# Up pairs of the last feed-forward block in seven block products

## What is computed

```python
def swiglu(h, w_gate, w_up, w_down):
    return (jax.nn.silu(h @ w_gate) * (h @ w_up)) @ w_down

h = modulate(rms_norm(x, norm_ffn2[i]), sh3, sc3)
x = x + 0.5 * gt3[:, None, :] * swiglu(h, ffn2_gate[i], ffn2_up[i], ffn2_down[i])
```

## Time and profile before

| | |
|---|---|
| median of 3 runs | 1440.79 us (1439.36 to 1442.40) |
| profiled execution, whole | 1442.35 us |
| its span | 1440.7 us |
| PE busy, 11790 matmuls | 1391.4 us, 97% |
| DVE busy | 976.9 us, 68% |
| ACT busy | 539.3 us, 37% |
| POOL busy | 77.4 us, 5% |

### The profile page before, as it was taken

The page is one execution under the profiler, slowest core; times in us unless marked ns, Lnnn a source line. Parts: engine busy times, 40 slices in busy tenths (PEclk is TensorE's granted clock), DMA queues, the critical chain, the costliest instruction groups (busy, mean ns, idle before and its releaser), DMA issues.

```text
span 1440.7 us, 28804 instructions
## 1 busy us (share of the span) xinstructions
PE 1391.4 (97%) x11790; PEld 1346.0 (93%) x11790; DVE 976.9 (68%) x1731; ACT 539.3 (37%) x797; POOL 77.4 (5%) x118
## 2 busy tenths in 40 slices
PE   6999999999999999999999998999999999999996
PEld 5899999999998999999899897999899999999996
DVE  5446775357546588998998997854554786456745
ACT  5323343224336222524233236422342344224433
POOL 6100000010001000000000000000000000000000
PEclk8999999999999999999999999999999999999998
DMA  9754646455364223213334443626312242223221
GB/s 323 229 180 146 210 150 205 146 166 146 97 206 143 87 88 93 89 60 103 128 123 147 147 156 126 212 89 199 110 41 91 74 134 89 96 81 117 90 87 60
DMA packets 132701, 189.49 MB, mean 132 GB/s; under 512 B 4621, under 2 KB 112545, under 8 KB 132386
## 3 DMA queue, kind: packets, MB, share of 16 engines
q1 hardware_dynamic: 111388, 112.54, 24.7%
q0 software_dynamic: 17136, 66.87, 13.8%
q10 hardware_dynamic: 4070, 8.57, 1.6%
HBM read 173.73 MB, written 15.18 MB: 131 GB/s over the span
## 4 chain that ended last, share of the span: by engine, by line
PE 82%; DVE 11%; ACT 3%; DMA 2%; issue 2%; POOL 0%; DVEq 0%; ACTq 0%; POOLq 0%
PE pu L642 47%; PE pu L817 13%; PE pu L806 11%; PE pu L658 3%; PE pg L679 2%; DVE w_lo L1667 2%; DMA work<-in_w_ada 1%; ACT w_hi L1214 1%; PE pg L1052 1%; DVE d L2087 1%; PE pg L715 1%; PE pg L1116 1%; DMA raw_a<-in_w_ada 1%; DVE w_lo L1956 1%; DVE work L2197 1%
## 5 line engine op out<-in xcount | busy, mean ns | idle before, releaser
L1667 DVE TENSOR_TENSOR w_lo<-raw,w_hi 128x1024 fp32r<-128x1024 f32 x152 | 186.1, 1225 | 259.2 <-ACT w_hi L1214 259.0
L1214 ACT CAST w_hi<-raw 128x1024 fp32r<-128x1024 f32 x152 | 158.8, 1046 | 402.0 <-PE pu L642 360.6
L642 PE MATMUL pu<-h_hi,w_hi 128*128 128x260 f32 x1408 | 288.5, 286 | 5.2 <-DVE w_lo L1667 3.6
L642 PE MATMUL pu<-h_hi,w_lo 128*128 128x260 f32 x1408 | 284.0, 283 | 0.0
L642 PE MATMUL pu<-h_lo,w_hi 128*128 128x260 f32 x1408 | 283.6, 283 | 0.0
L642 PEld LDWEIGHTS pu<-h_hi,w_hi 128*128 128x128 f32 x1408 | 217.5, 189 | 9.0 <-DVE w_lo L1667 5.3
L642 PEld LDWEIGHTS pu<-h_lo,w_hi 128*128 128x128 f32 x1408 | 217.4, 189 | 0.0
L642 PEld LDWEIGHTS pu<-h_hi,w_lo 128*128 128x128 f32 x1408 | 217.4, 189 | 0.0
L2087 DVE SCALAR_TENSOR_TENSOR d<-u,cw,d 128x512 f32<-128x512 f32 x240 | 163.1, 743 | 0.1
L642 PE MATMUL pu<-f_hi,w_hi 128*128 128x260 f32 x704 | 143.1, 284 | 0.9 <-DVE f_lo L2028 0.9
L642 PE MATMUL pu<-f_hi,w_lo 128*128 128x260 f32 x704 | 141.8, 283 | 0.0
(11 more groups left out here) (349 smaller groups left out, 2372.0 us busy)
## 6 DMA issues: line engine op xcount, KB each, us to landing
raw_a<-in_w_ada POOLq DMA_DIRECT2D x30, 1024.0 KB, 7.9
raw<-in_w_in SPq DMA_DIRECT2D x28, 1024.0 KB, 5.2
raw<-in_ffn_up SPq DMA_DIRECT2D x22, 1024.0 KB, 5.3
raw<-in_ffn_gate SPq DMA_DIRECT2D x21, 1024.0 KB, 5.3
raw<-in_ffn_down SPq DMA_DIRECT2D x16, 1024.0 KB, 5.1
gates_d<-sg ACTq DMA_DIRECT2D x24, 260.0 KB, 2.2
raw<-in_ffn_down SPq DMA_DIRECT2D x8, 768.0 KB, 4.4
work<-gates_d POOLq DMA_DIRECT2D x2, 2080.0 KB, 8.6
```

The source lines that it names most:

```text
L642: last = mm(pu[p][:, e, 0:HALF], w[p][:, k, :], m[:, k, e * HALF:(e + 1) * HALF], start=(k == 0 and j == 0), stop=(k == k_tiles - 1 and j ...
L1214: nc.scalar.copy(w_hi[p][:], raw[:, slot, :, p * P:(p + 1) * P]).then_inc(s_hi, 1)
L1667: V.tensor_tensor(w_lo[p][:], raw[:, slot, :, p * P:(p + 1) * P], w_hi[p][:].bitcast(F32), ALU.subtract).then_inc(s_lo, 1)
```

## The change

In groups 1 and 2 of the last feed-forward block (`which == 2`) the up pair too is made of seven block products. A turn is then 14 blocks (`2 * PAIR`), 168 matmuls: the gate pair in the four banks of `pu`, the up pair in the four of `pg`. The first feed-forward block keeps its turns of 11. With it:

- Weight sums of up pairs, and of the gate pairs of turns 2 to 4 of a group, are made by POOL; those of a group's first gate pair stay with DVE. The second half of `w_sums` holds the up pair's sums.
- The up pair's parts and result lie in `lb`. POOL multiplies `lb` by `sg` (Silu of gate) when both are whole, in the turn after; ACT's cast and DVE's `f_lo` follow in positions 0 to 2 of the next turn. For the last turn of a group they come behind all blocks, and the down unit starts with `GROUPS[g] - 2` tiles ready.
- DVE's first half-width sum of a turn waits for both POOL products of the turn before (`s_um`). Slab loads wait for POOL's sums as well.
- `unit_pair` gets `together`: that many k tiles run for both units, then the rest for unit 0, then the rest for unit 1 (6 for conv and yconv, 5 for the last feed-forward block, 8 as before for the first).
- In the last gate-up unit of group 0, in both feed-forward blocks, DVE multiplies gate and up before it splits the next weights.
- In yconv's loop `o_low` works on the tile of the same step and `o_gated` on the next one; one of each is moved in front of the loop.

The core of the diff:

```diff
+        def first_block(t):
+            return TURN * t if t < FFN2_TURN else TURN * FFN2_TURN + 2 * PAIR * (t - FFN2_TURN)
+
+        def pair_no(t, up=0):
+            return t if t < FFN2_TURN else FFN2_TURN + 2 * (t - FFN2_TURN) + up
+
+        def raw_quarter(t, up, m2, k2):
+
+            m2 = m2 if t < FFN2_TURN else 1 - m2
+            return raw[:, up, 4 * k2:4 * k2 + 4, m2 * P:(m2 + 1) * P]
+
+        def block_source(t, pos):
+
+            up, q = divmod(pos, PAIR) if t >= FFN2_TURN else (0, pos)
+            if q in SUM_OF:
+                return w_sums[:, 1 - up, SUM_OF[q]], s_wsum, 4 * pair_no(t, up) + SUM_OF[q] + 1
+            if t < FFN2_TURN:
+                return raw_block(pos), (s_graw if pos < U0A else s_uraw), 16 * (t + 1)
+            m2, k2 = {P1: (0, 0), P2: (0, 1), P4: (1, 1)}[q]
+            return raw_quarter(t, up, m2, k2), (s_uraw if up else s_graw), 16 * (t + 1)
+
+        def sum_of_weights(t, up, k):
+
+            a11, a12, a21, a22 = (raw_quarter(t, up, m2, k2) for m2 in range(2) for k2 in range(2))
+            w = w_sums[:, 1 - up]
+            return ((w[:, 0], a21, a22, ALU.add), (w[:, 1], w[:, 0], a11, ALU.subtract),
+                    (w[:, 2], a11, a21, ALU.subtract), (w[:, 3], a12, w[:, 1], ALU.subtract))[k]
@@ SP @@
                         sp.dma_start(raw[:, 0], cols(wg, r0 + 256 * it)).then_inc(s_graw, 16)
                         if it == 0:
                             sp.wait_ge(s_lo, n0)
+                        elif which == 1:
+                            sp.wait_ge(s_blo, TURN * t)
                         else:
-                            sp.wait_ge(s_blo, TURN * t)
+                            sp.wait_ge(s_blo, first_block(t - 1) + PAIR + P4 + 1)
+                            sp.wait_ge(s_wsum, 4 * pair_no(t - 1, 1) + 4)
                         sp.dma_start(raw[:, 1], cols(wu, r0 + 256 * it)).then_inc(s_uraw, 16)
-                    sp.wait_ge(s_blo, TURN * t + P4 + 1)
+                    sp.wait_ge(s_blo, first_block(t) + P4 + 1)
+                    if which == 2:
+                        sp.wait_ge(s_wsum, 4 * pair_no(t) + 4)
                     load(Lin(n0), 0, cols(wd, 0, r0=r0))
-                    sp.wait_ge(s_blo, TURN * (t + 1))
+                    if which == 1:
+                        sp.wait_ge(s_blo, TURN * (t + 1))
+                    else:
+                        sp.wait_ge(s_blo, first_block(t) + PAIR + P4 + 1)
+                        sp.wait_ge(s_wsum, 4 * pair_no(t, 1) + 4)
                     load(Lin(n0 + 2), 1, cols(wd, 256, r0=r0))
                     pair(Lin(n0 + 4), wd, 512, r0=r0)
@@ POOL @@
+            def add_weights(t, up):
+
+                for k in range(4):
+                    pool.wait_ge(s_wsum, 4 * pair_no(t, up) + k)
+                    if k == 0:
+                        pool.wait_ge(s_uraw if up else s_graw, 16 * (t + 1))
+                        if t > FFN2_TURN:
+                            pool.wait_ge(s_blo, first_block(t) if up else first_block(t - 1) + P3 + 1)
+                    out, a, b, op = sum_of_weights(t, up, k)
+                    nc.gpsimd.tensor_tensor(out, a, b, op).then_inc(s_wsum, 1)
+
+            def hidden(t, k):
+
+                pool.wait_ge(s_sg, 2 * t + k + 1)
+                pool.wait_ge((s_c2, s_c12)[k], pair_no(t, 1) + 1)
+                nc.gpsimd.tensor_tensor(lb[:, 1 - k, :], lb[:, 1 - k, :], sg[:, 1 - k, :], ALU.mult).then_inc(s_um, 1)
+
+            for g in (1, 2):
+                for it, t in turns(2, g):
+                    if it == 0:
+                        add_weights(t, 1)
+                    if it + 1 < TURNS:
+                        add_weights(t + 1, 0)
+                    hidden(t, 0)
+                    hidden(t, 1)
+                    if it + 1 < TURNS:
+                        add_weights(t + 1, 1)
+
 
@@ PE @@
+            def unit_pair(n, hi, lo, s, v, between=None, together=KT):
 
 
                 for p in range(2):
                     weights_and_psum(n + p, p)
-                for k in range(KT):
+                def rows(p, k):
+
+                    pe.wait_ge(s, v + k + 1)
+                    for j, (w, m) in enumerate(((w_hi, hi), (w_hi, lo), (w_lo, hi))):
+                        for e in range(2):
+                            last = mm(pu[p][:, e, 0:HALF], w[p][:, k, :], m[:, k, e * HALF:(e + 1) * HALF],
+                                      start=(k == 0 and j == 0), stop=(k == KT - 1 and j == 2))
+                    if k == KT - 1:
+                        last.then_inc(s_done, 1)
+
+                for k in range(together):
                     if between is not None:
                         between(k)
-                    pe.wait_ge(s, v + k + 1)
                     for p in range(2):
-                        for j, (w, m) in enumerate(((w_hi, hi), (w_hi, lo), (w_lo, hi))):
-                            for e in range(2):
-                                last = mm(pu[p][:, e, 0:HALF], w[p][:, k, :], m[:, k, e * HALF:(e + 1) * HALF],
-                                          start=(k == 0 and j == 0), stop=(k == KT - 1 and j == 2))
-                        if k == KT - 1:
-                            last.then_inc(s_done, 1)
+                        rows(p, k)
+                for p in range(2):
+                    for k in range(together, KT):
+                        rows(p, k)
 
+            def pairs_of_blocks(g):
+
+
+                for it, t in turns(2, g):
+                    for up in range(2):
+                        q, j = pair_no(t, up), first_block(t) + PAIR * up
+                        a0, a1, b0, b1 = (pg[:, b, 0:HALF] if up else pu[b // 2][:, b % 2, 0:HALF] for b in range(4))
+                        first, used = it == 0 and not up, it > 0 or (up and g == 2)
+                        if first:
+                            pe.wait_ge(s_evac[0], at[f"down2_{g}"] // 2)
+                        if used:
+                            pe.wait_ge(s_u3, q - 1)
+                            pe.wait_ge(s_c2, q - 1)
+                        product(j + P1, a0, h_block(h_hi, 0, 0), h_block(h_lo, 0, 0))
+                        product(j + P2, a1, h_block(h_hi, 1, 0), h_block(h_lo, 1, 0))
+                        if first:
+                            pe.wait_ge(s_evac[1], at[f"down2_{g}"] // 2)
+                            pe.wait_ge(s_tl, 8)
+                        if used:
+                            pe.wait_ge(s_v2, q - 1)
+                            pe.wait_ge(s_c12, q - 1)
+                        product(j + P6, b0, t_hi[:, 1], t_lo[:, 1])
+                        product(j + P5, b1, t_hi[:, 0], t_lo[:, 0])
+                        pe.wait_ge(s_p1, q + 1)
+                        product(j + P7, a0, t_hi[:, 2], t_lo[:, 2])
+                        pe.wait_ge(s_c11, q + 1)
+                        product(j + P4, a1, t_hi[:, 3], t_lo[:, 3])
+                        pe.wait_ge(s_u2, q + 1)
+                        product(j + P3, b0, h_block(h_hi, 1, 1), h_block(h_lo, 1, 1))
...
+                                pe.wait_ge((s_c2, s_c12)[c], end)
                             unit(Lin(at["down2_2"] + c), c % 2, f_hi, f_lo, GROUPS[g],
-                                 ready=(s_a, a0, GROUPS[g] - 1) if c == 0 else None)
+                                 ready=(s_a, a0, GROUPS[g] - 2) if c == 0 else None)
                             if c:
                                 y_transposes(c - 1)
                         continue
@@ ACT @@
+            def pair_turns(g):
+
+
+                def hidden(t, k):
+
+                    act.wait_ge(s_um, 2 * t + k + 1)
+                    nc.scalar.copy(f_hi[:, 2 * (t % TURNS) + k, :], lb[:, 1 - k, :]).then_inc(s_ahi, 1)
+
+                for it, t in turns(2, g):
+                    for pos in range(2 * PAIR):
+                        act.wait_ge(s_bd, first_block(t) + pos + 1)
+                        if pos % PAIR == P1:
+                            nc.scalar.copy(parts[pos // PAIR][0], (pg if pos else pu[0])[:, 0, 0:HALF]).then_inc(s_p1, 1)
+                        if pos + 4 < 2 * PAIR:
+                            block_hi(it, t, pos + 4)
+                        elif it + 1 < TURNS:
+                            block_hi(it + 1, t + 1, pos + 4 - 2 * PAIR)
+                        elif pos in (2 * PAIR - 3, 2 * PAIR - 1):
+                            k = (pos - 2 * PAIR + 3) // 2
+                            split_hi(Lin(at[f"down2_{g}"] + k), k, 0)
+                        if pos == P3:
+                            act.wait_ge(s_c2, pair_no(t) + 1)
+                            af(sg[:, 1, :], sg[:, 1, :], ACT.Silu).then_inc(s_sg, 1)
+                        if pos == PAIR:
+                            act.wait_ge(s_c12, pair_no(t) + 1)
+                            af(sg[:, 0, :], sg[:, 0, :], ACT.Silu).then_inc(s_sg, 1)
+                        if it and pos < 2:
+                            hidden(t - 1, pos)
+                hidden(t, 0)
+                hidden(t, 1)
```

(58 more changed lines are left out.)

71 lines of the change are left out of this document (41 added, 30 removed).

## The result

| | before | after |
|---|---|---|
| median of the runs compared, us | 1440.74 (1438.66 to 1444.43) | 1444.55 (1442.36 to 1447.13) |
| ratio to before, 95% interval | 1 | 1.0024 [1.0017, 1.0031] |
| span of the profiled execution, us | 1440.7 | 1442.3 |

The account below looks back on a forecast made before the run. PE's matmuls were taken to bound the kernel: span 1440.7 - 11.5 (matmuls) - 4.4 (small edits) + 4.8 (stalls) + 0.6 (tail) = 1430.2, so a forecast median of 1430.3 us, 0.73% faster; range 1424 to 1440.

Parts of the forecast that it names:

- 96 x 0.120 = 11.5 us off: Last feed-forward block: twelve fewer matmuls in each of 8 turns, 0.120 us each, take 11.5 us off PE's work.
- rival A: Last block: POOL collisions cost nothing, DVE's waits stay under its slack (hold up to 0.95 us); 1425.5 us, chance 0.19.
- rival D: Turn start: DVE's first sum waits for POOL's second product; nothing at hold 1.05, 3 us from 1.3; no separate chance.
- rival E: Last block: matmuls don't go away or pairs wait for PSUM banks; no such wait seen; "other" had chance 0.03.
- POOL's operation, 1.1 us: Last block: a two-input POOL sum or product takes 1.1 us, between 0.88 and 1.30; ten per full turn, 11 us.
- One engine at a time on the path: SBUF: POOL's reads and DVE's two-SBUF-input operations block each other; hold 1.05 us (0.83 to 1.25), half-width sums overlap.
- The full turn of 21.7 and the stall of 2.4 us per group: Last block: holds make DVE need 21.7 us per full turn against PE's 20.1; stalls 2.4 us per group, 4.8 for both.
- the slack of 2.85: Last block: DVE may lag 2.85 us behind in its block splits before PE stops.
- The account by turns: Stalls within a group: first turn no lag, second costs 0.1 us, third 1.6, last 0.7.
- The small edits, 4.4 us: PE gaps at conv, yconv, yconv-to-ygla, first and last feed-forward blocks: gains sum to 4.4 us (3.0 to 4.8).
- Tail, 0.6 us: End of each group: last turn's gating runs behind the last product, 0.3 us per group, 0.6 total (0 to 1.2).
- C: Rival: DVE and POOL together bound the turn, 23.7 us, splits over 1.5, PE waiting for w_lo; 1443 to 1450, chance 0.12.

Follow-up runs that it names:

- e3: Changed kernel with POOL's sums and products in the last block replaced by their signals (first four sums by a MEMSET each); 1425.06 us, 0.9891.
- e5: Changed kernel with each POOL sum and product in the last block replaced by three constant writes that read nothing; 1425.2 us, 0.9884.
- e4: Changed kernel with all sums and products computed on DVE, none on POOL, the eight sums spread between the blocks; 1426.03 us, 0.9896.
- e7: Changed kernel, complete, with POOL's gate sums held back, one for each of products 6 to 9 of a turn; 1443.49 us, 1.0016.

## Why the prediction was wrong

The sum said 1430.2 for the span; it was 1442.3. The stalls and tails were 20.4 us and not 5.4 (+15.0), and ahead of the last block 7.3 came back and not 4.4 (-2.9): +12.1. The median came out 0.65 above the profiled execution (1443.9), where it had been 1.56 below it: +2.2.

- **What bounds the kernel, and 96 x 0.120 = 11.5 us off.** Right. With POOL idle a turn is 20.16 us and the whole 1425.06, against 1425.5 in rival A (the second partly by luck, as said under e3).
- **ACT has cover; the new waits (rival D) and PSUM (rival E) cost nothing.** Right: e5 keeps every wait, with POOL as late as in the kernel after, and PE shows none of them.
- **POOL's operation, 1.1 us, ends 0.88 and 1.30.** It is 1.27 where it starts first, inside but at the end, and 1.60 to 1.70 in the mean beside DVE, where 1.0 to 1.2 was to be seen. The estimate from the Trainium skill (GPSIMD Engine Reference, "Elementwise — side-by-side cycle accounting"), 1.2, was the nearer one.
- **One engine at a time on the path.** Right, with a hold of 1.09 against 1.05, splits at 1.04 on average (0.8 to 1.1 forecast) and half-width sums unchanged. The rule of the Trainium skill (SBUF — State Buffer, "Who interferes with whom") agrees here: 1.78 for a 0.69 operation beside reads, and 0.69 beside writes only (e5).
- **The full turn of 21.7 and the stall of 2.4 us per group. This step failed,** and not by the size of the hold: with 1.10 the same walk gives the 7 us that stand in the prediction, and the stalls and tails were 20.4. It failed in two ways. First the two low halves, which I had put at 0.61 each, outside the holds. They take their turn behind POOL as well (1.78 each), and each uses up a POOL operation with no half-width sum under it: 10 x 1.70 + 6 x 0.97 = 22.8 for the turn, where 22.7 to 23.0 was measured, and the formula with 1.10 gives 22.2. Then the place. I had spread the ten operations over eleven blocks, with a peak of 3.0 us of lag. They ran from 1172.45 to 1189.69, broken only by the 0.78 us that POOL waited for the gate slab, over eight splits and two low halves. That is 17.2 us in which PE could have used up eight products, 11.5: a lag of 5.7, and less the slack of 2.85 it is 2.9 us of stall in a turn (2.5 to 2.9 measured in three of the four full turns).
- **Sum or place?** The sum over a turn gives much the same 22.8, but it lets slack take the first of it. The second turn of group 2 speaks for the place: DVE had caught up ahead of it (idle for 0.30 and 0.75 us at 1311.51 and 1313.25, until ACT's cast), so by the sum, 2.6 over PE's turn, its slack of 2.85 would have covered it, and it lost 2.5. No run tested this by thinning out the stretch.
- **The account by turns.** The first turn of a group was to have no lag, and that of group 2 lost 1.6, where POOL's up sums met the splits and the residual. The last turns lost 2.1 each, for 0.7.
- **The clock.** No term of the sum stood for it. A stall of 1.4 and one of 2.1 us in a row were followed by 3.4 us at the lower level, 1.57 us more; and ahead of the last block time at the lower level went away that I had not counted, 3.4 us by the windows, for the 2.9 that are left of 7.3 less 4.4.
- **The small edits, 4.4 us.** The gaps came out as said: 1.07 in front of 463.47 (with 0.38 of new idle time elsewhere, so a gain of 0.32), 0.83 for 1.26 (with 0.39 of new idle time in front of 927.59), 0.37 for 1.78, none at 948 and 121.
- **Tail, 0.6 us.** Too high. In e5, where POOL's results come as late as in the kernel after, the last turn up to the first residual is 26.89 in both groups, where before less twelve matmuls is 28.23 - 1.44 = 26.79: 0.1 for each group. In e4, where DVE is just in time, PE waits 0.16 us for tile 7's low half.
- **The rivals.** C happened, in time (1443 to 1450), sign and PE's waits for w_lo in every middle turn. Its turn of 23.7 and its splits of over 1.5 us did not quite: three of four full turns are 22.7 to 23.0, and the splits are at 1.04 in the mean, with single ones up to 1.8. I had put its point of decision at a hold of 1.25, or 1.15 with losses at each hand-over; it decided at 1.10. The chance of 0.12 was too low because the whole case rested on slack that was nearly used up at my own figures, 21.7 us asked of 20.1: any term left out could only go one way.
- **What I did not ask:** whether to give the work to POOL at all. By the rows of before, DVE had 14.8 of 20.1 us; with its own ten operations back it is 20.4 (e4), which the slack still takes, and is cheaper than POOL's holds.

## What to carry to other kernels

Before moving an operation with two SBUF inputs from a busy DVE to POOL, price it as the hold it puts on DVE (here 0.84 to 0.96 us for 128x512) and not as POOL's idle time; if that is more than DVE's own 0.60, keep it. Walk the densest stretch of a turn, with every operation in it that can collide, the rare ones too, and hold that against the slack, before the sum over the turn. Read the granted clock behind each new stall on PE: here it fell behind waits of 1.39 and 2.06 us in one turn, and stayed at 1.00 behind 1.38, 0.95 and 0.44 in the same turn of e7.

## What was not expected of the hardware

- A two-input POOL operation of 128x512 takes 1.27 us where it starts first, 1.61 behind one of DVE's two-input operations, and they alternate one for one at 1.70.
- POOL that only writes (MEMSETs of 0.527 us, back to back) leaves such a DVE operation at 0.69; POOL that reads makes it 1.78.
- Sums of half width with one input in PSUM stay at 0.41 to 0.42 beside POOL in all of these kernels.
- The clock's lower level can follow short gaps on PE: 3.4 us of it behind waits of 1.39 and 2.06 us. Ahead of the last block, what the clock fell short of 1.00 summed to 3.4 us between 1044 and 1056 before, and to 1.7 in the same stage when the products there were regrouped.
